# Scores of a gated recurrent layer: six levels of halving against three levels of quartering

## The chip, the cores and the metric

The kernel runs on one core of one Trainium2 chip. The metric is the device time of one execution in microseconds, lower is better; the median of three runs is 2374.85 us (2374.75 to 2374.86). Besides these runs there is one profiled execution, whose trace the profile and all rows below come from.

## The reference, cut to what matters

Two layers on 512 prompt frames and 32 sample frames of width 2048, 16 heads of 128. The first layer is an attention layer, the second a gated linear recurrence; the change lies in the second. Each layer has an input projection to four times the width and an output projection. In the recurrent layer a head's output is a sum over earlier frames, each weighted by a product of query and key and by the decay between the two frames:

```python
def hgrn2_chunk(S, inp):
    q, k, v, g = inp
    b = jnp.cumsum(g, axis=2)                                    # log decay, summed over the chunk
    o = jnp.einsum('bhtk,bhkv->bhtv', q * jnp.exp(b), S)         # what the state adds
    ...
    decay = jnp.exp(jnp.minimum(bs[:, :, :, :, None] - bs[:, :, :, None, :], 0.0))
    diag = jnp.einsum('bhaik,bhajk,bhaijk->bhaij', qs, ks, decay) * tri
    scores = off + jnp.einsum('bhaij,ac->bhaicj', diag, jnp.eye(n, dtype=diag.dtype))
    o = o + jnp.einsum('bhts,bhsv->bhtv', scores.reshape(bn, h, c, c), v)
    S_new = jnp.exp(b_last)[..., None] * S + jnp.einsum('bhsk,bhsv->bhkv', k * jnp.exp(jnp.minimum(b_last[:, :, None] - b, 0.0)), v)
    return S_new, o
```

The chunking is an identity of the mathematics; the kernel takes chunks of 128 frames. The exponent between a query and a key must never be positive, so a score can't be split into one factor of the query and one of the key over the whole chunk; it is split around a frame that lies between the two.

## The kernel before

**Projections.** Everything is kept transposed, 128 features on the partitions and 544 = 512 + 32 frames in the free dimension. A projection tile is 16 blocks of contraction; each is split in a rounded part and a remainder of weights and activations (`w_hi`, `w_lo`, `act_hi`, `act_lo`), and three products of 272 columns times two are summed (line 474). A tile is two halves of 8 blocks. One head needs four tiles, so eight halves, u = 0 to 7. Weights come in by SP's queue into a ring of four (`w_raw`); ACT rounds them (`hi`), DVE takes the difference (`lo`, line 1143), three halves ahead.

**The loop.** In the layer's loop over heads h = 0 to 14, PE computes half u of head h + 1 and after it the piece `rec_stage(h, u)` of head h. The last head, 15, has no half beside it; the first contraction blocks of the output projection, listed in `LAST_FILL`, are put between its pieces. DVE and ACT walk through the same u: first the weight split, then the evacuation of a projection tile (`evacuate`), then their part of head h (`rec_dve`, `rec_act`), then the start of head h + 1 (`rec_next`, and at u = 7 `rec_distances` and `rec_decays`). Each engine works in its written order; semaphores order the engines among each other.

**The levels.** The scores of a chunk are made by halving. At level m (64, 32, 16, 8, 4, 2) blocks of 2m frames are cut in two; the second half has the queries, the first the keys, and the decay is split at the first half's last frame. For a level DVE makes the differences of the summed log decays (`level(h, i, 0)`, lines 1265 and 1266, two instructions of 272 elements, 256 at the levels 64 and 32), ACT takes the exponential in place (`level_exp`, 544 or 512 elements), DVE multiplies with keys and queries (`level(h, i, 1)`, lines 1271 and 1272), and PE multiplies the two in full f32: one matmul of 64 columns for each of the four prompt chunks (line 595), and from m = 16 down one of 16 columns for the sample frames (line 599). A matmul in f32 stands as two records in the trace. `put` copies a level's scores under a mask into the score matrix `A`, with four or five COPY_PREDICATED (lines 1285 and 1292). The level m = 1 needs no matmul by chunk: products of neighbours, summed over the partitions by a matmul with ones (`pair`).

**What orders them.** Two buffers each for differences and products alternate (`dl`, `xl`), and two banks of PSUM, `M[1]` and `M[0]`, for the scores. PE's levels stand at u = 0 (m = 64), 1 (32), 2 (16), 3 (8 and 4) and 4 (2); at u = 5 PE multiplies `A` with the values. `r_x` tells PE that a level's products are there, `r_lev` tells DVE that its scores are, and `r_put` tells that they lie in `A`. The key and query products of the first two levels of a head are made at u = 7 of the head before, in `rec_distances`.

**Further names.** `own` is the diagonal score, with a remainder `own_lo` that PE waits for at u = 2; `kd` are the decayed keys for the state, turned by PE at u = 1; `S` is the state; `gate_r` the output gate. GpSimd (POOL) builds masks at the start, sums squares, and at the end of each layer takes the remainders `act_lo` of the first blocks of the output projection (line 450), while the last head is still in work.

Of the kernel before, what the change touches and what calls it, by code (L numbers as in the profile page):

```python
# [66 lines left out]
LEVELS = [64, 32, 16, 8, 4, 2, 1]  # L67
MASK_COL = {m: 64 * i for i, m in enumerate(LEVELS)}
# [37 lines left out]
def encoder_step(nc, x_prompt, x_sample, cache_k, cache_v, state_hgrn, norm_w, w_in, w_out, q_norm_w, k_norm_w,  # L106
# [4 lines left out]
    with ExitStack() as ctx:  # L111
# [26 lines left out]
        level_mask = sb("level_mask", [P, 64 * len(LEVELS)])  # L138
# [59 lines left out]
        qs, kk, qe, kd = c(T), c(T), c(T), c(T)  # L198
        eb = c(T)
        gate_r = g_tmp_r = c(T)  # L200
        dl = [c(T) for _ in range(2)]
        xl = [c(T) for _ in range(2)]
# [4 lines left out]
        o_cp, o_sq = xl  # L207
        o_hi, o_lo = [work_r(n, (4 * 2 + 2 + i) * T, T) for i, n in enumerate(("o_hi", "o_lo"))]
# [3 lines left out]
        pair = dl[0][:, 0:HT]  # L212
        pair_hi = work_r("pair_hi", (4 * 2 + 3) * T, HT)
        pair_lo = work_r("pair_lo", (4 * 2 + 3) * T + HT, HT)
# [74 lines left out]

        NL = len(LEVELS)  # L290

# [97 lines left out]
        def _(pool):  # L389
# [29 lines left out]
            for m in LEVELS:  # L419
                v = level_mask[:, MASK_COL[m]:MASK_COL[m] + 64].rearrange("p (b j) -> p b j", j=m)  # L420

                ch.done(pool.affine_select(out=v, in_=v, pattern=[[-2 * m, 64 // m], [0, m]], base=0,
                                           channel_multiplier=1, compare_op=ALU.is_ge, fill=0.0))
                ch.wait()
                ch.done(pool.affine_select(out=v, in_=v, pattern=[[2 * m, 64 // m], [0, m]], base=m - 1,
# [37 lines left out]
        def _(pe):  # L463
# [124 lines left out]
            def rec_level(h, i, bank):  # L588

                m = LEVELS[i]  # L590
                pe.wait_ge(r_x, h * NL + (i + 1))
                x = xl[i % 2]
                for b in range(NB):
                    rhs = x[:, b * P:(b + 1) * P].rearrange("p (b j) -> p b j", j=2 * m)[:, :, m:2 * m]
                    mm = pe.matmul(M[bank][:, b * 64:(b + 1) * 64], x[:, b * P:(b + 1) * P], rhs,  # L595
                                   start=True, stop=True)
                if m <= SAMPLE // 2:
                    rhs = x[:, SEQ:T].rearrange("p (b j) -> p b j", j=2 * m)[:, :, m:2 * m]
                    mm = pe.matmul(M[bank][:, 256:256 + SAMPLE // 2], x[:, LAST:T], rhs, start=True, stop=True)
                mm.then_inc(r_lev, 1)  # L600

            def rec_stage(h, u):
                if u == 2:
                    pe.wait_ge(kd_rows_cleared, 1)
                if u == 0:
                    if not (isinstance(h, int) and h == 0):
                        pe.wait_ge(r_orstd, h)
                    rec_level(h, 0, 1)
                elif u == 1:
# [6 lines left out]
                    rec_level(h, 1, 0)  # L616
# [520 lines left out]
        def _(dve):  # L1137
# [110 lines left out]
            def level(h, i, part):  # L1248
# [13 lines left out]
                if part == 0:  # L1262
                    if i >= 2:
                        dve.wait_ge(r_x, h * NL + (i - 1))
# [301 lines left out]
```

## Time and profile before

| | us |
|---|---|
| median of three runs | 2374.85 |
| the profiled execution's own time | 2374.45 |
| its span, first to last instruction | 2372.7 |
| PE busy in the span | 2333.4 (98%) |
| DVE busy | 1252.3 (53%) |
| ACT busy | 1021.1 (43%) |
| POOL busy | 96.2 (4%) |
| matmuls of the projections, line 474, three groups of 5120 | 1081.5 + 1063.1 + 1060.0 |
| matmuls of the levels, line 595, 768 records | 99.4 |
| the same for the sample frames, line 599, 128 records | 22.4 |

A record's duration reaches past the start of the next one, since matmuls are pipelined; so the sums of line 474 exceed the span, and what a matmul costs PE is read from one start to the next. DVE's and ACT's instructions overlap by about a tenth of a microsecond in the same way. Of the span, the part from 1237 to 2134 us is the loop of the recurrent layer, and 2134 to 2190 us its last head.

### The profile page before, as it was taken

To read this page: it belongs to the slowest core of one execution; us is meant where nothing else is said; L and a number is where in the kernel's file an instruction comes from. 1 tells how busy PE (TensorE), PEld (TensorE's weight loads), DVE (VectorE), ACT (ScalarE), POOL (GpSimd) and SP (SyncE) were. 2 spreads that over 40 slices of the span, in tenths; PEclk is the share of its full clock that TensorE was granted. 3 is DMA by queue.
4 is the path that set the end of the run, shared out by engine and by line. 5 is a ranking of instruction groups with operands and counts; after the bars stand their busy time and mean duration, and the time that the engine had idled before them with its cause. 6 is when DMAs were issued, how large, how long until landed. Compare 5 with 4: busy or idle time off the path is not lost. (4 is left out here: it accounts for less than half of the span.)

```text
span 2372.7 us, 46285 instructions
## 1 busy us (share of the span) xinstructions
PE 2333.4 (98%) x18457; PEld 2310.9 (97%) x18457; DVE 1252.3 (53%) x2278; ACT 1021.1 (43%) x1386; POOL 96.2 (4%) x95
## 2 busy tenths in 40 slices
PE   7999999999999999999999999999999999998999
PEld 6999999999999999899999999999999999997999
DVE  6444444444444444432357777777777777776221
ACT  5444444444444444532344444444444444444221
POOL 6000000000000000310100000000000000003000
PEclk9999999999999999999999999999999999998999
DMA  7333222222222222254532222222222222212542
GB/s 236 100 87 87 85 85 85 85 85 85 85 85 85 85 85 83 62 156 116 143 91 75 74 73 69 71 73 74 69 71 73 74 74 74 74 48 57 149 118 78
DMA packets 388088, 211.29 MB, mean 89 GB/s; under 512 B 9091, under 2 KB 378294, under 8 KB 388022
## 3 DMA queue, kind: packets, MB, share of 16 engines
q1 hardware_dynamic: 340182, 181.19, 26.8%
q10 hardware_dynamic: 47872, 29.64, 4.1%
q8 instruction: 22, 0.36, 0.1%
q14 instruction: 12, 0.10, 0.0%
HBM read 186.41 MB, written 24.38 MB: 89 GB/s over the span
## 5 line engine op out<-in xcount | busy, mean ns | idle before, releaser
L474 PE MATMUL psum<-act_hi,w_hi 128*128 128x272 f32 x5120 | 1081.5, 293 | 13.5 <-DVE act_lo L1152 5.3
L474 PE MATMUL psum<-act_hi,w_lo 128*128 128x272 f32 x5120 | 1063.1, 289 | 0.0
L474 PE MATMUL psum<-act_lo,w_hi 128*128 128x272 f32 x5120 | 1060.0, 289 | 0.0
L1143 DVE TENSOR_TENSOR w_lo<-w_raw,w_hi 128x1024 fp32r<-128x1024 f32 x320 | 400.5, 1252 | 859.3 <-ACT w_hi L785 859.2
L474 PEld LDWEIGHTS psum<-act_hi,w_hi 128*128 128x128 f32 x5120 | 805.7, 189 | 16.6 <-DVE act_lo L1152 4.4
L474 PEld LDWEIGHTS psum<-act_lo,w_hi 128*128 128x128 f32 x5120 | 807.9, 189 | 0.0
L474 PEld LDWEIGHTS psum<-act_hi,w_lo 128*128 128x128 f32 x5120 | 803.4, 190 | 0.0
L785 ACT ACTIVATE w_hi<-w_raw 128x1024 fp32r<-128x1024 f32 x320 | 338.0, 1057 | 680.8 <-PE psum L474 634.7
L785 ACT ACTIVATE work<-work 128x544 f32<-128x544 f32 (+2 forms) x368 | 261.4, 723 | 313.0 <-DVE work L1266 198.7
L785 ACT ACTIVATE work<-psum 128x512 f32<-128x512 f32 (+5 forms) x256 | 111.3, 483 | 148.8 <-PE psum L465 115.1
L450 POOL TENSOR_TENSOR act_lo<-full,act_hi 128x544 fp32r<-128x544 f32 x24 | 37.1, 1548 | 1905.5 <-DVE act_lo L1152 1876.5
L595 PE MATMUL psum<-work 128*128 128x64 f32 x768 | 99.4, 273 | 3.6 <-DVE work L1272 3.6
L595 PEld LDWEIGHTS psum<-work 128*128 128x128 f32 x768 | 95.6, 195 | 4.0 <-issue 2.3
L1160 DVE TENSOR_TENSOR Y<-psum,rstd_x 128x544 f32<-128x544 f32 x126 | 90.3, 717 | 8.7 <-ACT rstd_x L785 6.3
L785 ACT ACTIVATE work<-work,one_c 128x544 f32<-128x544 f32 (+1 forms) x80 | 78.2, 978 | 2.1
L1535 DVE TENSOR_TENSOR work<-psum,work 128x544 f32<-128x544 f32 x32 | 23.2, 724 | 92.6 <-PE psum L474 92.6
L785 ACT ACTIVATE work<-Y 128x1088 f32<-128x1088 f32 x64 | 56.3, 880 | 21.9 <-PE psum L577 21.9
L785 ACT ACTIVATE sp_hi<-work 128x1376 fp32r<-128x1376 f32 x32 | 43.4, 1355 | 48.1 <-DVE work L1196 46.6
L1285 DVE COPY_PREDICATED work<-level_mask,psum 128x64 f32<-128x64 int32 x384 | 60.9, 238 | 0.0
L465 PE MATMUL psum<-ident,work 128*128 128x128 f32 (+2 forms) x289 | 48.5, 277 | 6.6 <-DMA work<-in_hgrn_norm_w 3.8
L439 POOL TENSOR_TENSOR work<-work 128x544 f32<-128x544 f32 x32 | 47.1, 1472 | 169.0 <-ACT work L785 168.3
L1272 DVE TENSOR_TENSOR work<-work 128x272 f32<-128x272 f32 (+1 forms) x112 | 50.3, 449 | 0.0
(205 smaller groups left out, 1710.3 us busy)
## 6 DMA issues: line engine op xcount, KB each, us to landing
w_raw<-in_w_in SPq DMA_DIRECT2D x256, 512.0 KB, 4.0
w_raw<-in_w_out SPq DMA_DIRECT2D x64, 512.0 KB, 6.3
out<-work ACTq DMA_DIRECT2D x48, 256.0 KB, 2.4
x_residual<-work ACTq DMA_DIRECT2D x32, 272.0 KB, 3.8
work<-x_residual SPq DMA_DIRECT2D x32, 272.0 KB, 3.0
full<-in_x_prompt SPq DMA_DIRECT2D x3, 1024.0 KB, 11.5
work<-in_cache_k ACTq DMA_DIRECT2D x16, 128.0 KB, 2.3
work<-in_cache_v ACTq DMA_DIRECT2D x16, 128.0 KB, 4.1
```

The lines of the kernel that those rows point to most:

```text
L439: pool.tensor_tensor(sq_sum, sq_sum, squares, ALU.add).then_inc(x_summed, 1)
L450: pool.tensor_tensor(act_lo[:, k, :], full[:, k, :], act_hi[:, k, :].bitcast(F32), ALU.subtract).then_inc(act_lo_ready, 1)
L465: return pe.matmul(out, in_, ident[0:n, 0:n], is_transpose=True, start=True, stop=True, **kw)
L474: mm = pe.matmul(acc[par][:, j, :], w[:, slot, k % KH, :], a[:, k, j * HT:(j + 1) * HT], start=(k == 0 and n == 0), stop=(k == KT - 1 and ...
L595: mm = pe.matmul(M[bank][:, b * 64:(b + 1) * 64], x[:, b * P:(b + 1) * P], rhs, start=True, stop=True)
L785: return nc.scalar.activation(out, in_, f, **kw)
L1143: dve.tensor_tensor(w_lo[:, slot], w_raw[:, slot], w_hi[:, slot].bitcast(F32), ALU.subtract).then_inc(lo_ready, 1)
L1160: dve.tensor_tensor(Y[:, j, :].rearrange("p (a t) -> p a t", a=2), acc[j % 2], rstd_x[:].rearrange("p (a t) -> p a t", a=2), ALU.mult).the ...
L1272: dve.tensor_tensor(x2, cut(qs)[1], d2, ALU.mult).then_inc(r_x, 1)
L1285: ins = dve.copy_predicated(dst, msk, src)
L1535: dve.tensor_tensor(x_new[par].rearrange("p (a t) -> p a t", a=2), acc[par], x_old[par].rearrange("p (a t) -> p a t", a=2), ALU.add).then_ ...
```

## The change

The levels become groups of quartering: blocks of 4m frames with m = 32, 8, 2 are cut in four parts. The parts' keys are decayed to the end of their own part, once; the queries come in three sets, one for each of the three ends inside the block: 3m queries behind the first end, 2m behind the second, m behind the third, 6m columns for 4m frames. One matmul of 192 columns per chunk (48 for the sample frames) gives the scores of all three sets for a group; three groups with 24 + 4 records take the place of six levels with 48 + 8 records per head. The pairs of neighbours stay, made directly from `cum`, `qs` and `kk`.

```diff
-LEVELS = [64, 32, 16, 8, 4, 2, 1]
+GROUPS = [32, 8, 2]
+GROUP_COLS = 192
+BUF = T + 6 * T // 4
...
+            def rec_group(h, i):
+                n = in_group(i)[1]
+                pe.wait_ge(r_x, h * NL + (i + 1))
+                xk, xq = key_part(i), query_part(i)
                 for b in range(NB):
+                    at = (b % 2) * 256
+                    mm = pe.matmul(M[b // 2][:, at:at + GROUP_COLS], xk[:, b * P:(b + 1) * P],
+                                   xq[:, b * GROUP_COLS:(b + 1) * GROUP_COLS], start=True, stop=True)
...
+                ch.done(func(xk, xk, ACT.Exp))
+                func(xq, xq, ACT.Exp).then_inc(r_dexp, 1)
...
+            def group(h, i, part):
...
+                    ends = blocks(c)[:, :, m - 1:m].broadcast_to([P, 4 * segs, m])
+                    ch.done(dve.tensor_tensor(blocks(xk), ends, blocks(c), ALU.subtract))
+                    for b in range(3):
+                        end = c[:, :, (b + 1) * m - 1:(b + 1) * m].broadcast_to([P, segs, (3 - b) * m])
+                        ins = dve.tensor_tensor(xq[:, :, q_at[b]:q_at[b + 1]], c[:, :, (b + 1) * m:4 * m], end, ALU.subtract)
...
+                    ch.done(dve.tensor_tensor(xk[:, :, 0:3 * m], k[:, :, 0:3 * m], xk[:, :, 0:3 * m], ALU.mult))
+                    for b in range(3):
+                        v = xq[:, :, q_at[b]:q_at[b + 1]]
+                        ins = dve.tensor_tensor(v, q[:, :, (b + 1) * m:4 * m], v, ALU.mult)
...
+            def put(h, i, *between):
+                for b in range(3):
...
+                        dve.memset(tick, 0.0)
...
+                    on = msk[:, b, :].unsqueeze(1).unsqueeze(3).broadcast_to([P, NB, segs, w])
+                    ins = dve.copy_predicated(dst[:, :, :, (b + 1) * m:4 * m], on, scores[:, :, :, q_at[b]:q_at[b + 1]])
```

Each group's scores fill both `M[0]` and `M[1]`, so a group on PE waits until the one before lies in `A`. The three copies of `put` overlap in `A`, so each waits for the one before it, behind a MEMSET of one element that carries the wait or behind another instruction (the gate). The masks of POOL at the start become six short ones instead of fourteen, with 63 columns instead of 448. The buffers of the first group lie over `o_cp`, so `rec_distances` now waits for the head's output (`o_ready`) at its first instruction instead of ahead of its products. The order of the pieces on PE becomes: group 32 at u = 0, nothing at u = 1 and 2, group 8 at u = 3, group 2 at u = 4.

On PE, in the loop at u = 3, the levels m = 8 and m = 4 stood one behind the other, before:

```order
L591 REGISTER_ALU [waits r_own_scores_times_v]
L595 MATMUL psum<-work 128x64 [waits r_x]
L595 MATMUL psum<-work 128x64 x3
L599 MATMUL psum<-work 128x16
L591 REGISTER_ALU [waits r_scores_put]
L595 MATMUL psum<-work 128x64 [waits r_x]
L595 MATMUL psum<-work 128x64 x3
L599 MATMUL psum<-work 128x16
```

The same place now, up to the next half:

```order
L611 REGISTER_ALU [waits r_own_scores_times_v]
L615 MATMUL psum<-work 128x192 [waits r_x]
L615 MATMUL psum<-work 128x192 x3
L618 MATMUL psum<-work 128x48
L499 REGISTER_ALU
```

One group of wider matmuls stands where two levels stood, and the wait for `r_put` (named `r_scores_put`) between them is gone.

On DVE, in the loop at u = 4, behind the weight split (`w_lo`) and the evacuation (`Y`), before:

```order
L1160 TENSOR_TENSOR Y<-psum,rstd_x 128x544 [waits half_done]
L1285 COPY_PREDICATED work<-level_mask,psum 128x8x8 [waits r_level_scores,r_scores_put,consts_ready]
L1285 COPY_PREDICATED work<-level_mask,psum 128x8x8 x3
L1292 COPY_PREDICATED work<-level_mask,psum 128x2x8
L1268 REGISTER_ALU
L1271 TENSOR_TENSOR work<-work 128x136x2 [waits r_level_scores,r_dexp]
L1272 TENSOR_TENSOR work<-work 128x136x2
```

The same place now; line 1413 is the gate, line 1304 the differences of the pairs:

```order
L1177 TENSOR_TENSOR Y<-psum,rstd_x 128x544 [waits half_done]
L1304 TENSOR_TENSOR work<-work 128x272 [waits r_level_scores]
L1327 MEMSET small 128x1 [waits r_level_scores,r_scores_put,consts_ready]
L1334 COPY_PREDICATED work<-level_mask,psum 128x16x24
L1340 COPY_PREDICATED work<-level_mask,psum 128x24
L98 REGISTER_ALU
L1413 TENSOR_TENSOR work<-Y,work 128x544 [waits r_gate_sig,dve_chain]
L1334 COPY_PREDICATED work<-level_mask,psum 128x16x16
L1340 COPY_PREDICATED work<-level_mask,psum 128x16
L98 REGISTER_ALU
L1332 MEMSET small 128x1 [waits dve_chain]
L1334 COPY_PREDICATED work<-level_mask,psum 128x16x8
```

The products of level m = 2 stood behind the copies and PE waited for them; the products of group 2 now stand ahead, at the end of u = 3, and PE's group 2 waits for the last of these copies.

On DVE at u = 7, from the head's output (`full`) to the products of the next head's first level, before:

```order
L1398 TENSOR_TENSOR full<-work 128x544
L1265 TENSOR_TENSOR work<-work 128x4x64 [waits r_cum]
L1266 TENSOR_TENSOR work<-work 128x4x64
L1303 TENSOR_TENSOR work<-work 128x128 x4
L1303 TENSOR_TENSOR work<-work 128x32
L1265 TENSOR_TENSOR work<-work 128x8x32
L1266 TENSOR_TENSOR work<-work 128x8x32
L1268 ISA [waits o_ready,r_qk]
```

The same place now, with the products (line 1293 and below):

```order
L1445 TENSOR_TENSOR full<-work 128x544
L1286 TENSOR_TENSOR work<-work 128x512 [waits o_ready,r_cum]
L1289 TENSOR_TENSOR work<-work 128x4x96
L1289 TENSOR_TENSOR work<-work 128x4x64
L1289 TENSOR_TENSOR work<-work 128x4x32
L1356 TENSOR_TENSOR work<-work 128x128 x4
L1356 TENSOR_TENSOR work<-work 128x32
L1292 ISA [waits r_qk]
L1293 TENSOR_TENSOR work<-work 128x4x96 [waits r_dexp]
```

The differences of a second level, which stood between the first level's differences and its products, are gone; only the differences for `kd` are left between, and the wait for `o_ready` moved to the front.

## Rows read from the trace of the kernel before

**Rows 1.** Busy time by stretch, the loop: stretch and length, PE, PEld, DVE, ACT, POOL, clock.

```profile
1290.00:2140.00 850.00, 847.95 (x6862) 845.29 (x6861) 612.63 (x1461) 396.00 (x571) 0.00 (x0) 1.00 0.24 71
```

**Rows 2.** All waits of PE from 1225 to 2190 us: total, times, longest.

```profile
PE psum L628 <- DVE own_lo L1333: 5.2, 1, 5.2
PE psum L595 <- DVE work L1272: 3.6, 2, 2.1
PE psum L474 <- DVE act_lo L1152: 1.6, 1, 1.6
PE psum L660 <- DVE o_lo L1377: 1.4, 1, 1.4
```

**Rows 3.** Timeline of PE in the loop: start, us, line, operands, columns, records.

```profile
1613.56 0.39 PE L622 MATMUL psum<-work 128*128 128x128 f32 x2
1613.78 1.00 PE L595 MATMUL psum<-work 128*128 128x64 f32 x8
...
1621.61 1.00 PE L595 MATMUL psum<-work 128*128 128x64 f32 x8
1622.44 0.35 PE L599 MATMUL psum<-work 128*128 128x16 f32 x2
1622.64 1.08 PE L595 MATMUL psum<-work 128*128 128x64 f32 x8
...
1623.76 0.50 PE L474 MATMUL psum<-act_hi,w_hi 128*128 128x272 f32 x2
...
1629.86 1.00 PE L595 MATMUL psum<-work 128*128 128x64 f32 x8
...
1658.53 1.00 PE L595 MATMUL psum<-work 128*128 128x64 f32 x8
1659.34 0.50 PE L474 MATMUL psum<-act_hi,w_hi 128*128 128x272 f32 x2
```

**Rows 4.** Timeline of PE, a matmul of 512 columns in f32 between the layers.

```profile
1199.25 1.02 PE L719 MATMUL psum<-work,ones_r 128*128 128x512 f32 x2
1200.11 0.30 PE L720 MATMUL psum<-work,ones_r 128*128 128x32 f32 x2
```

**Rows 5.** Timeline of DVE in the loop, u = 4.

```profile
1622.90 1.22 DVE L1143 TENSOR_TENSOR w_lo<-w_raw,w_hi 128x1024 fp32r<-128x1024 f32 x1 [2.79 <-ACT w_hi L785]
...
1624.67 0.61 DVE L1285 COPY_PREDICATED work<-level_mask,psum 128x64 f32<-128x64 int32 x4
1625.19 0.17 DVE L1292 COPY_PREDICATED work<-level_mask,psum 128x16 f32<-128x16 int32 x1
1625.28 0.43 DVE L1271 TENSOR_TENSOR work<-work 128x272 f32<-128x272 f32 x1
1625.63 0.44 DVE L1272 TENSOR_TENSOR work<-work 128x272 f32<-128x272 f32 x1
```

**Rows 6.** Waits of DVE for itself in the layer: total, times, longest.

```profile
DVE work L1239 <- DVE work L1237: 2.3, 15, 0.2
```

**Rows 7.** Timeline of DVE and ACT at u = 7, around the first level.

```profile
1651.60 0.42 DVE L1265 TENSOR_TENSOR work<-work 128x256 f32<-128x256 f32 x1
...
1654.18 0.42 DVE L1272 TENSOR_TENSOR work<-work 128x256 f32<-128x256 f32 x1
...
1652.38 0.63 ACT L785 ACTIVATE work<-work 128x512 f32<-128x512 f32 x1 [4.20 <-DVE work L1266]
```

**Rows 8.** Costliest groups of the page, ACT's weight rounding: busy, mean ns, idle before.

```profile
L785 ACT ACTIVATE w_hi<-w_raw 128x1024 fp32r<-128x1024 f32 x320 | 338.0, 1057 | 680.8 <-PE psum L474 634.7
```

**Rows 9.** Timeline of the last head: POOL, DVE, PE.

```profile
2152.01 2.83 POOL L450 TENSOR_TENSOR act_lo<-full,act_hi 128x544 fp32r<-128x544 f32 x2 [2.16 <-ACT act_hi L785]
...
2153.57 1.85 DVE L1333 TENSOR_TENSOR own_lo<-work,own_hi 128x544 fp32r<-128x544 f32 x1
...
2169.99 1.27 PE L595 MATMUL psum<-work 128*128 128x64 f32 x8 [1.56 <-DVE work L1272]
```

**Rows 10.** Busy time in the last head behind the wait of 5.2 us, columns as rows 1.

```profile
2155.00:2162.00 7.00, 6.53 (x33) 6.33 (x34) 5.42 (x19) 2.41 (x4) 0.91 (x1) 0.61 0.52 151
```

More of the change, by code:

```diff
@@ L197, in encoder_step @@
         cum = c(T)
-        qs, kk, qe, kd = c(T), c(T), c(T), c(T)
+        qs, kk, qe = c(T), c(T), c(T)
         eb = c(T)
         gate_r = g_tmp_r = c(T)
-        dl = [c(T) for _ in range(2)]
-        xl = [c(T) for _ in range(2)]
+        at_bufs = c.at
+        assert 2 * BUF == 5 * T
+        bufs = [c(BUF) for _ in range(2)][::-1]
+        kd = bufs[1][:, 0:T]
+        tick = small[:, 7, 2:3]
         A = c(SEQ + SAMPLE)
@@ L206, in encoder_step @@
         S = c(6 * P).rearrange("p (b d) -> p b d", b=6)
-        o_cp, o_sq = xl
-        o_hi, o_lo = [work_r(n, (4 * 2 + 2 + i) * T, T) for i, n in enumerate(("o_hi", "o_lo"))]
+        o_cp, o_sq = [work[:, at_bufs + i * T:at_bufs + (i + 1) * T] for i in range(2)]
+        o_hi, o_lo = [work_r(n, at_bufs + (2 + i) * T, T) for i, n in enumerate(("o_hi", "o_lo"))]
         own = lse
@@ L1295, in rec_distances @@
             def rec_distances(h):
                 dve.wait_ge(r_cum, h + 1)
-                level(h, 0, 0)
+                if not (isinstance(h, int) and h == 0):
+                    dve.wait_ge(o_ready, h + H)
+                group(h, 0, 0)
                 for b in range(5):
@@ L1304, in rec_distances @@
                     ins.then_inc(r_kdx, 1) if b == NB else ch.done(ins)
-                level(h, 1, 0)
                 dve.wait_ge(r_qk, h + 1)
-                if not (isinstance(h, int) and h == 0):
-                    dve.wait_ge(o_ready, h + H)
-                level(h, 0, 1)
+                group(h, 0, 1)
                 dve.wait_ge(r_kde, h + 1)
                 dve.tensor_tensor(kd, kd, kk, ALU.mult).then_inc(r_kd, 1)
-                level(h, 1, 1)
             def rec_dve(h, u):
@@ L1333, in rec_dve @@
                     dve.tensor_tensor(own_lo, own, own_hi.bitcast(F32), ALU.subtract).then_inc(r_own_lo, 1)
-                    level(h, 4, 0)
+                    group(h, 1, 1)
                 elif u == 3:
@@ L1342, in rec_dve @@
                                       ).then_inc(r_own_v, 1)
-                    put(h, 2, 1)
-                    level(h, 4, 1)
-                    level(h, 5, 0)
+                    group(h, 2, 0)
                     dve.wait_ge(r_upd, h + 1)
```

207 lines of the change are left out of this document (111 added, 96 removed).

## The prediction

> **What bounds the kernel now.** I read the busy time by stretch first. In the loop of the recurrent layer PE is busy for 847.95 of 850 us at the full clock, DVE for 612.63, ACT for 396.00 [rows 1]. Then PE's waits: from the layer's first head to its end there are four entries, 11.8 us in all [rows 2], and all lie in the last head: of 1240 to 2134 us the same view is empty. So in the loop PE waits for nobody: a microsecond taken from PE in a head is a microsecond of the kernel as long as DVE and ACT keep ahead of it, and one added to DVE or ACT is free up to their lead. The last head is the opposite: there PE waits for DVE, and DVE's order counts. Hence three questions: what a head's scores cost PE, whether the lead holds in the loop, and what the last head does.
>
> **PE: the levels go.** A matmul in f32 is two records, so a level is 8 records of 64 columns, and from m = 16 down 2 more of 16. From start to start the first level takes 1659.34 - 1658.53 = 0.81 us [rows 3], the second repeats it. At u = 3 the first of the two takes 1622.64 - 1621.61 = 1.03 and the second 1623.76 - 1622.64 = 1.12; the levels at u = 2 and u = 4 repeat 1.03. A head: 2 x 0.81 + 3 x 1.03 + 1.12 = 5.83 us.
>
> **PE: the groups come.** A head now has 3 x 8 records of 192 columns and 2 x 2 of 48. No row has 192 columns in f32, so I price it between neighbours: 64 columns 0.10 each (0.81 / 8), 128 columns 0.11 ((1613.78 - 1613.56) / 2) [rows 3], 512 columns 0.43 ((1200.11 - 1199.25) / 2) [rows 4]. From 128 to 512 columns the slope is 0.32 / 384 = 0.83 ns per column; from 64 to 128 it is far flatter, so below 128 something other than the columns sets the pace, and at 128 the columns have caught up (128 x 0.83 = 0.107). For 192: 0.11 + 64 x 0.83 ns = 0.164. Bounds: 0.160 if only columns count; and, if what fills the 64-column record stays and columns are added to it, 0.104 + 128 x 0.83 ns = 0.211. I take 0.164, because 128 and 512 columns [rows 3, 4] lie on one line through almost zero, and the upper bound contradicts the row of 128 columns. The two records of 48 take the 0.20 of the two of 16 (1622.64 - 1622.44): 64 columns cost no more. A head: 24 x 0.164 + 2 x 0.20 = 4.34 us. The columns rise by half (1536 to 2304 prompt columns), the time falls, because half of the 64-column record was not columns.
>
> The saving is 5.83 - 4.34 = 1.49 us a head, in 15 heads of the loop 22.4 us. The changes between f32 and the other matmuls stay as many per head: each u keeps a piece in f32 except that u = 1 and u = 2 keep theirs without a level.
>
> **DVE and ACT: the work stays about equal.** DVE's price from start to start [rows 5]: 64 masked elements (0.52 / 4 = 0.13), 16 in 0.09, 272 in 0.35, on one line 0.065 + 1.05 ns per element. Before, a head has 28 + 1 instructions of 256 or 272 (29 x 0.35 = 10.1) and 28 copies (24 x 0.13 + 4 x 0.09 = 3.5), together 13.6 us. After: per group differences of 544, 408, 272 and 136 elements (0.64 + 0.49 + 0.35 + 0.21 = 1.69) and products of 408, 408, 272, 136 (1.54), three groups 9.7; pairs 3 x 0.35 = 1.05; copies per group of 384, 256 and 128 (0.47 + 0.33 + 0.20), for two groups 24, 16 and 8 besides (0.25): 3.5; MEMSETs and waits for its own copies (0.15 each, 2.3 / 15) [rows 6] about 1.5. Together 15.7, 2 us more on an engine that has (850 - 612.63) / 14, or 17 us a head, free. What counts is where. ACT: seven exponentials of some 540 elements become six of 408 and 816 and one of 272, elements 3744 to 3944: nothing.
>
> **Where the lead is thinnest.** First, u = 4. PE's group 2 overwrites both banks and so waits for the last copy of group 8. In times of the trace before: DVE starts the weight split at 1622.90 and its copies could start at 1624.67 [rows 5]. Now come the pairs' differences 0.35, a MEMSET 0.07, copies 0.47 + 0.09, a wait and the gate 0.15 + 0.64, copies 0.33 + 0.08, wait and MEMSET 0.22, copies 0.20 + 0.17: 2.8, done at 1627.4. PE ends the half of u = 3 at 1621.61, then group 8 (1.31 + 0.20), then the half of u = 4, 1629.86 - 1623.76 = 6.10: 1629.2. Lead 1.8 us, no wait.
>
> Second, the first group of the next head. The chain on DVE ran from 1651.60 to the last product's end at 1654.18 + 0.42 = 1654.60 [rows 7], PE came at 1658.53 [rows 3]: 3.9 us. Now: the wait for its own output 0.15, differences of 512, 384, 256, 128 (1.60), to 1653.4; then ACT: 512 elements last 0.63 [rows 7], 1024 last 1.06 [rows 8], 0.84 ns per element, so 384 and 768 are 0.52 + 0.85 with 0.1 overlapped, plus 0.1 to start: 1654.8. DVE fills only 0.9 of that with `kd`, waits 0.5, and multiplies for 1.47: 1656.3. Lead 2.2 us, no wait in the loop. The diagonal scores of u = 2 don't wait longer than before: `own_lo` now follows four differences (1.69) where a masked copy and two products stood (1.2).
>
> **The last head.** There nothing covers the second chain: PE waited 2.1 us for the first level [rows 2] and will wait 1.7 more. Then POOL is at work for `act_lo`, and DVE's instructions with two inputs slow down: `own_lo` took 1.85 us there [rows 9] against 0.64 by the line above. Before, four level instructions stood ahead of the weight split at u = 1 and two more before `own_lo`; now the gate and four differences stand there. Counting one and a half microseconds for each under POOL, `own_lo` comes about 2.5 us earlier, so the wait of 5.2 us shrinks to some 2.5. Later group 2 waits for copies that follow the weight split, where before the last products did, with a wait of 1.56 [rows 9]: PE comes there some 3 us earlier and waits about 2.5 us longer. Waits lower the clock: 0.61 of full speed behind the 5.2 us [rows 10]. I sum the last head to 0 with 4 us either way, its own 1.49 used up.
>
> **Sum.** Span 2372.7 - 22.4 = 2350.3; around it the profiled execution has 1.75 us (2374.45), and the median of the runs lies 0.4 above that: 2374.85 - 22.4 = **2352.5 us**. The shorter mask work of POOL at the start I cost at nothing, since PE and DVE wait there for the input frames.
>
> **The rivals.** *A record's fixed part stays under wide columns* (0.211): a head costs 24 x 0.211 + 0.40 = 5.46, saves 0.37, in 15 heads 5.5: 2369. Against it stands the row of 128 columns (0.11, not 0.157); 5%.
>
> The Trainium skill ("TensorE: Matmul & The Clock Gate", section "Part 3: Packing small matmuls — row/col tiling") says that a weight load overlaps running matmuls only where the row groups differ. All loads here use all rows, so by that rule each load would stand in front of its matmul, which is this rival and its 2369. The rows of 128 and 512 columns disagree with it; the same page's section "LDWEIGHTS (loading the stationary operand)" gives a load as columns / 1.2 ns, 107 ns for 128, which is close to the 0.10 of the narrow records, as a floor and not as an addend.
>
> *DVE is late at u = 4 in every head.* Masks broadcast along two axes and scores read in four-dimensional pieces have no row; if the copies cost 4 times my price per element, the 816 elements take 2.6 us longer, against a lead of 1.8: PE waits 0.8 a head. The clock then falls: at 0.61 over 7 us the loss is 0.39 x 7 = 2.7 us. 15 x (0.8 + 2.7) = 52 against 22.4: 2374.85 + 30 = 2405, slower. It decides from three times the price on. For it: no row has such a copy. Against: the masked copies of 64 and of 16 elements lie on the line of the plain ones. 7%, of it 2% with waits too short to turn the sign.
>
> *The last head eats part of it*: `own_lo` doesn't come earlier, the two later waits stay, and the clock is low longer: 2.5 + 1.7 + 2.7 = 7 us, 2359.5; 8%.
>
> **How the numbers follow.** Forecast 80%, with its own range 2348 to 2357 (price 0.160 gives 1.4 us less, last head 4 either way). With the last head's case, 88%: range 2347 to 2361; the two other cases lie outside. Two runs of this kernel differ by far less than 0.2% (4.7 us), which I take as what can be told from no change. Faster: 80 + 8 + 5 = 93%; slower 5%; between 2%.
>
> **What would show it.** Right: 384 records of 192 columns at 0.164 from start to start, 4.3 us of scores per head on PE, no wait of PE in the loop, 1.5 us less from head to head, PE's busy time lower by some 23 us, the last head's waits moved from `own_lo` to the first group and group 2. Wrong: records of 192 columns at 0.2 or more; PE waiting in the loop for line 1340 (copies) or 1296 (products); a granted clock below 1.00 in the loop; copies of 384 elements above 1 us.

## The result and the profile after

The changed kernel's median is 2343.26 us (2341.09 to 2343.76), beside 2374.8 us of the kernel before: a ratio of 0.9867, 95% interval 0.9855 to 0.9878. The direction was right; the time lies below the range's low end of 2347. The profiled execution, the fastest of its four, has a span of 2339.1 us, 33.6 less than before.

Where the 33.6 us lie is read from two rows of PE's timeline, the first and the last turn of `v` (transposing matmuls, line 465 before, 485 after): they stand ahead of head 0's pieces and ahead of the last head's, fifteen heads apart. Columns: start, us, engine, line, operands, columns, records. Before:

```profile
1230.40 0.71 PE L465 MATMUL psum<-ident,Y 128*128 128x128 f32 x5
...
2133.68 0.71 PE L465 MATMUL psum<-ident,Y 128*128 128x128 f32 x5
```

After, with the groups of one head between them:

```profile
1226.02 0.71 PE L485 MATMUL psum<-ident,Y 128*128 128x128 f32 x5
...
1582.55 1.46 PE L615 MATMUL psum<-work 128*128 128x192 f32 x8
1583.72 0.55 PE L494 MATMUL psum<-act_hi,w_hi 128*128 128x272 f32 x2
...
1590.34 0.50 PE L494 MATMUL psum<-act_hi,w_hi 128*128 128x272 f32 x2
...
1598.15 0.50 PE L494 MATMUL psum<-act_hi,w_hi 128*128 128x272 f32 x2
...
1604.25 1.46 PE L615 MATMUL psum<-work 128*128 128x192 f32 x8
1605.55 0.32 PE L618 MATMUL psum<-work 128*128 128x48 f32 x2
...
1611.79 1.46 PE L615 MATMUL psum<-work 128*128 128x192 f32 x8
...
2100.92 0.71 PE L485 MATMUL psum<-ident,Y 128*128 128x128 f32 x5
```

| us of the profiled execution | before | after | difference |
|---|---|---|---|
| up to the first turn | 1230.40 | 1226.02 | -4.4 |
| fifteen heads of the loop | 903.28 | 874.90 | -28.4 |
| behind the last turn, to the end | 239.02 | 238.18 | -0.8 |

A head takes 58.33 us instead of 60.22, 1.89 less; the prediction had 1.49. At u = 3 eight records of 192 columns take 1605.55 - 1604.25 = 1.30, so 0.1625 each. The loop, as rows 1 (stretch and length, PE, PEld, DVE, ACT, POOL, clock, and DMA share and GB/s, which aren't used):

```profile
1260.00:2080.00 820.00, 820.00 (x6467) 817.50 (x6467) 623.19 (x1333) 390.44 (x563) 0.00 (x0) 1.00 0.26 75
```

PE is still the bound, at the full clock; DVE's busy time is 44.3 us a head (623.19 / 820 x 58.33) instead of 43.4 ([rows 1], 612.63 / 850 x 60.22), 0.9 more where the prediction had 2. PE's waits from the layer's first head to the end of its last, as [rows 2]:

```profile
PE psum L644 <- DVE own_lo L1381: 4.1, 1, 4.1
PE psum L615 <- DVE work L1296: 3.8, 1, 3.8
PE psum L615 <- DVE work L1340: 3.0, 1, 3.0
PE psum L494 <- DVE act_lo L1169: 1.7, 1, 1.7
PE psum L674 <- DVE o_lo L1424: 0.9, 1, 0.9
```

All lie in the last head, none in the loop; together 13.5 us, where it was 11.8. The two thin leads, on DVE's timeline: the end of the first group's chain at u = 7 (as [rows 7]) and the copies of group 8 at u = 4 (as [rows 5]).

```profile
1579.29 1.09 DVE L1296 TENSOR_TENSOR work<-work 128x384 f32<-128x384 f32 x3
...
1607.67 0.59 DVE L1334 COPY_PREDICATED work<-level_mask,psum 128x384 f32<-128x384 int32 x1
...
1608.15 0.18 DVE L1340 COPY_PREDICATED work<-level_mask,psum 128x24 f32<-128x24 int32 x1
...
1609.75 0.16 DVE L1340 COPY_PREDICATED work<-level_mask,psum 128x8 f32<-128x8 int32 x1
```

The last copy ends at 1609.91 and PE comes to group 2 at 1611.79: a lead of 1.9 (predicted 1.8). The copy of 384 elements takes 0.48 from start to start (predicted 0.47). The first group's products end at 1580.38, PE comes at 1582.55: 2.2 (predicted 2.2).

So three differences ask for a cause: 0.40 us a head more than predicted, the start, and the last head, where little changed though its waits did.

### The profile page after: what moved, and what is told of

The parts are those of the page before. It is cut to its first block, busy times and chain, and to the rows that moved or that the text cites. A ratio compares the mean times of both kernels' runs of the same rounds, so it can differ in the third digit from the quotient of the medians.

```text
span 2339.1 us, 45080 instructions
## 1 busy us (share of the span) xinstructions
PE 2300.3 (98%) x18009; PEld 2277.7 (97%) x18009; DVE 1272.3 (54%) x2150; ACT 1018.9 (44%) x1386; POOL 91.8 (4%) x87
## 4 chain that ended last, share of the span: by engine, by line
PE 93%; DVE 2%; ACT 2%; issue 1%; ACTq 0%; DVEq 0%
PE psum L494 79%; PE psum L615 3%; PE psum L485 2%; PE psum L590 1%; PE psum L572 1%; PE psum L540 1%; PE psum L566 1%; ACT work L799 1%; PE psum L661 1%; ACT act_hi L799 1%; PE psum L640 1%; PE psum L663 0%; PE psum L522 0%; PE psum L521 0%; PE psum L546 0%
## 5 line engine op out<-in xcount | busy, mean ns | idle before, releaser
L799 ACT ACTIVATE work<-work 128x544 f32<-128x544 f32 (+6 forms) x368 | 256.5, 726 | 335.4 <-DVE work L1289 191.2
L615 PE MATMUL psum<-work 128*128 128x192 f32 x384 | 72.3, 332 | 6.8 <-DVE work L1296 3.8
L1334 DVE COPY_PREDICATED work<-level_mask,psum 128x384 f32<-128x384 int32 x144 | 68.2, 474 | 4.9 <-PE psum L618 2.2
L615 PEld LDWEIGHTS psum<-work 128*128 128x128 f32 x384 | 63.4, 193 | 7.3 <-issue 4.0
L799 ACT ACTIVATE sp_hi<-work 128x1376 fp32r<-128x1376 f32 x32 | 43.4, 1355 | 48.1 <-DVE work L1213 46.7
L1296 DVE TENSOR_TENSOR work<-work 128x408 f32<-128x408 f32 (+1 forms) x144 | 57.7, 457 | 0.0
L1289 DVE TENSOR_TENSOR work<-work 128x408 f32<-128x408 f32 (+1 forms) x144 | 56.4, 447 | 0.0
```

The source lines that it names most:

```text
L615: mm = pe.matmul(M[b // 2][:, at:at + GROUP_COLS], xk[:, b * P:(b + 1) * P], xq[:, b * GROUP_COLS:(b + 1) * GROUP_COLS], start=True, stop= ...
L799: return nc.scalar.activation(out, in_, f, **kw)
L1289: ins = dve.tensor_tensor(xq[:, :, q_at[b]:q_at[b + 1]], c[:, :, (b + 1) * m:4 * m], end, ALU.subtract)
L1296: ins = dve.tensor_tensor(v, q[:, :, (b + 1) * m:4 * m], v, ALU.mult)
L1334: ins = dve.copy_predicated(dst[:, :, :, (b + 1) * m:4 * m], on, scores[:, :, :, q_at[b]:q_at[b + 1]])
```

## Experiments

### Why a head saves 1.89 and not 1.49

Theory P is the prediction's own reading: a level costs what lies between its first record and the next matmul of a half. Theory H: that stretch leaves something out, since a half takes 6.10 us behind a piece in f32 and 6.02 behind the piece at u = 5, which ends in records of 272 columns like the half's own (means over the heads in both kernels). The data type alone doesn't make this difference: behind the pieces at u = 2 and u = 6, which end in records of the half's own kind (one record for a matmul) with 32 columns, a half takes 6.10 as well. To tell the theories apart, the piece at u = 0 was taken out of either kernel's loop (shown for the changed one; in the kernel before it is `rec_level(h, 0, 1)`). The last product but one of the half ahead gives `r_lev` (`early`), and the copies read other data, so the scores of the first group are left out. The kernels of this section and the next ran once each; their times from head to head are means over fifteen heads.

```diff
                 if u == 0:
                     if not (isinstance(h, int) and h == 0):
                         pe.wait_ge(r_orstd, h)
-                    rec_group(h, 0)
+                    if isinstance(h, int):
+                        rec_group(h, 0)
...
+                            if early is not None and (k, n, j) == (ks[-1], 2, 0):
+                                mm.then_inc(early, 1)
...
+                if i == 0 and not isinstance(h, int):
+                    scores = work[:, 4 * T:4 * T + NB * GROUP_COLS].rearrange("p (n x) -> p n x", n=NB)
```

> The kernel before without the matmuls of level m = 64 in the loop (the copies then put other data into A in their place); the half ahead of it gives the semaphore. So u = 0 has no piece in f32 between two halves. Read is the time from head to head (60.22 us in the kernel before). Theory P (the prediction's reading: a level costs what lies between its first record and the first matmul of the half behind it): 0.81 less, 59.41. Theory H (a piece in f32 costs more than that, because the half behind it takes 6.10 from its first to its last start and 6.02 where no piece in f32 stands ahead, as at u = 5): 0.89 less, 59.33, and the half behind the empty place takes 6.02.

> The changed kernel without the matmuls of group m = 32 in the loop (the copies take other data), the same edit on the other side. Read is the time from head to head (58.33 us in the changed kernel). The prediction's price, 8 x 0.164: 1.31 less, 57.02. Theory P read from the changed kernel's own trace (1.16 from the first record to the half behind it): 57.17. Theory H (1.16 and the longer half behind it, 6.16 against 6.02): 1.30 less, 57.03. If H holds on both sides, the prediction had the groups' price right and the levels' too low.

The timeline of PE in the kernel before: the half ahead of the level at u = 0 (line 474), the turn behind the next half (line 465), and the first matmuls of the halves at u = 2 and u = 3:

```profile
1592.23 0.50 PE L474 MATMUL psum<-act_hi,w_hi 128*128 128x272 f32 x2
...
1605.22 0.71 PE L465 MATMUL psum<-ident,work 128*128 128x128 f32 x5
...
1606.58 0.50 PE L474 MATMUL psum<-act_hi,w_hi 128*128 128x272 f32 x2
...
1615.51 0.50 PE L474 MATMUL psum<-act_hi,w_hi 128*128 128x272 f32 x2
```

The same without the level, with the first and the last turn:

```profile
1231.13 0.71 PE L465 MATMUL psum<-ident,Y 128*128 128x128 f32 x5
...
1587.71 0.50 PE L474 MATMUL psum<-act_hi,w_hi 128*128 128x272 f32 x2
...
1599.82 0.71 PE L465 MATMUL psum<-ident,work 128*128 128x128 f32 x5
...
2121.41 0.71 PE L465 MATMUL psum<-ident,Y 128*128 128x128 f32 x5
```

The two halves with the level take 1605.22 - 1592.23 = 12.99, without it 1599.82 - 1587.71 = 12.11: 0.88, though only 0.81 lie between first record and next half [rows 3]. From head to head it is (2121.41 - 1231.13) / 15 = 59.35, 0.87 less than 60.22: nearer to H's 0.89 than to P's 0.81. The changed kernel without its first group:

```profile
1227.36 0.71 PE L485 MATMUL psum<-ident,Y 128*128 128x128 f32 x5
...
2082.66 0.71 PE L485 MATMUL psum<-ident,Y 128*128 128x128 f32 x5
```

855.30 / 15 = 57.02, 1.31 less than 58.33: the prediction's 8 x 0.164 to the hundredth, where P from this kernel's rows (1583.72 - 1582.55 = 1.17) is 0.14 short. So the groups were priced right and the levels too low.

How much too low, records of 96 and of 64 columns tell (each matmul of 192 cut in two, in three):

```diff
-                    mm = pe.matmul(M[b // 2][:, at:at + GROUP_COLS], xk[:, b * P:(b + 1) * P],
-                                   xq[:, b * GROUP_COLS:(b + 1) * GROUP_COLS], start=True, stop=True)
+                    for n0 in range(0, GROUP_COLS, 64):
+                        mm = pe.matmul(M[b // 2][:, at + n0:at + n0 + 64], xk[:, b * P:(b + 1) * P],
+                                       xq[:, b * GROUP_COLS + n0:b * GROUP_COLS + n0 + 64], start=True, stop=True)
```

> The changed kernel with each score matmul of 192 columns cut into two of 96 with the same keys. Columns stay, records double (from 24 to 48 per head besides the sample frames'). Theory floor (a record of up to some 128 columns costs 0.104 whatever it holds, the reason for the change's gain): 48 x 0.104 = 5.0 in place of 24 x 0.1625 = 3.9, 1.1 us more per head, 16 us in the loop, about 2358 to 2361. Theory columns (only columns cost): no change, within 2 us of the changed kernel.

> The changed kernel with each score matmul of 192 columns cut into three of 64, columns next to each other. Theory floor: 72 x 0.104 = 7.5 in place of 3.9, 3.6 us more per head, 54 us in the loop, about 2396 to 2400, slower than the kernel before, so that quartering with narrow matmuls would lose. Theory columns: no change. It also tells whether the 0.115 from record to record of the levels m = 4 and below came from their strided columns: then 0.104 here.

PE's timeline with 96 columns, the turns and u = 0:

```profile
1227.80 0.71 PE L485 MATMUL psum<-ident,Y 128*128 128x128 f32 x5
...
1593.08 1.92 PE L616 MATMUL psum<-work 128*128 128x96 f32 x16
1594.78 0.50 PE L494 MATMUL psum<-act_hi,w_hi 128*128 128x272 f32 x2
...
2124.58 0.71 PE L485 MATMUL psum<-ident,Y 128*128 128x128 f32 x5
```

And with 64:

```profile
1228.75 0.71 PE L485 MATMUL psum<-ident,Y 128*128 128x128 f32 x5
...
1610.12 2.79 PE L616 MATMUL psum<-work 128*128 128x64 f32 x24
1612.72 0.50 PE L494 MATMUL psum<-act_hi,w_hi 128*128 128x272 f32 x2
...
2165.75 0.71 PE L485 MATMUL psum<-ident,Y 128*128 128x128 f32 x5
```

The heads take 59.79 and 62.47 us, 1.46 and 4.14 more than 58.33, and the kernels 2366.1 and 2409.86 us, the second slower than before. With 24 x 0.1625 = 3.90 taken away and 48 or 72 records put in, a record of 96 costs (3.90 + 1.46) / 48 = 0.112 and one of 64 costs (3.90 + 4.14) / 72 = 0.112. "Only columns cost" is out, and so is my floor of 0.104, by which 2358 to 2361 and 2396 to 2400 were expected. The pieces at u = 0 show why I read too little: 8, 16 and 24 narrow records take 0.81 [rows 3], 1.70 and 2.60 up to the next half, 0.112 for each further record and a fixed 0.09 less; the half behind gives that back. The single records of the trace show where. At u = 0 of the kernel before, the level's records start 0.110 to 0.112 apart, but the second only 0.056 behind the first, and the half 0.084 behind the last; within the half the second record then starts 0.211 behind the first, where 0.125 is its step. So 0.08 or 0.09 of the level's time stand within the half.

The levels that no experiment took out cost the same. From the first matmul of the half at u = 2 to that of the half at u = 3 there were 1615.51 - 1606.58 = 8.93, and now, with ten narrow records gone and nothing in their place, 1598.15 - 1590.34 = 7.81. Over all heads (means of fifteen, from half to half):

| us | u = 0 | u = 1 | u = 2 | u = 3 | u = 4 | u = 5 to 7 |
|---|---|---|---|---|---|---|
| before | 6.90 | 7.46 | 8.93 | 8.25 | 7.14 | 21.08 |
| after | 7.27 | 6.62 | 7.81 | 7.54 | 7.54 | 21.08 |
| narrow records out | 8 | 8 | 10 | 20 | 10 | 0 |
| records of 192 and of 48 columns in | 8 + 0 | 0 | 0 | 8 + 2 | 8 + 2 | 0 |

At u = 2 that is 1.11 for ten records, 0.111 each, where the prediction read 1.03 for the same level. At u = 1 it is 0.84 for eight, and 0.89 with the 0.05 or 0.06 that the half there has become longer behind the records of 192 columns (6.16 instead of 6.10). Inside both levels of u = 3 the records start 0.112 apart; the 0.115 read there holds a first step of 0.139, behind a record of 16 columns. In the cut groups the columns lay next to each other, so 0.112 needs no stride to explain it.

### The lead at u = 4

```diff
                     pairs(h, 0)
+                    if not isinstance(h, int):
+                        for n in range(6):
+                            ch.done(dve.tensor_tensor(spare[:], cum[:, 0:384], cum[:, 0:384], ALU.subtract))
+                            ch.wait()
                     put(h, 1, gate_out)
```

> The changed kernel with two more instructions on DVE at u = 4 of every head in the loop, ahead of the copies of group 8, each 384 elements and a wait for itself, together about 1.2 us. Theory lead (the last copy is done 1.9 us before PE comes to group 2): no wait of PE in the loop, head to head 58.33, time within the changed kernel's runs. Rival: the lead is smaller than it looks, because DVE's later work of the head comes later too and another place waits: more than 58.4 from head to head.

> The same with six such instructions, about 3.7 us. Theory lead: DVE is 1.8 us late at group 2 in every head and PE waits for the copies. The prediction's rival of that kind priced a wait with a low clock behind it, 0.39 of 7 us or 2.7 us: 1.8 + 2.7 = 4.5 us a head, 67 us in all, about 2411. Without a fall of the clock: 1.8 a head, 27 us, about 2370. Rival: the wait shifts DVE and PE against each other and other waits follow: more than 70 us.

With two, a head takes 58.33 as without (2344.25 us in all) and PE has no wait in the loop: the lead is more than those 1.2 us. With six, 2372.81 us. PE's waits in the loop:

```profile
PE psum L616 <- DVE work L1341: 24.5, 15, 1.6
```

Busy time by stretch there, columns as above:

```profile
1300.00:2100.00 800.00, 778.75 (x6117) 773.61 (x6116) 633.69 (x1340) 367.77 (x530) 0.00 (x0) 1.00 0.25 73
```

And the turns on PE's timeline:

```profile
1227.72 0.71 PE L486 MATMUL psum<-ident,Y 128*128 128x128 f32 x5
...
2131.01 0.71 PE L486 MATMUL psum<-ident,Y 128*128 128x128 f32 x5
```

A head takes 60.22: 1.89 more, against 1.8 of a late DVE. PE waits for the copies once in each of 15 heads, 1.6 us each (24.5 of the 15 x 1.89 = 28.4 us show as waits), and the granted clock stays at 1.00. So the rival of a late DVE was priced wrongly: its 2.7 us of low clock per head did not come with a wait of this length, twice its 0.8. Being 1.8 us late in every head would have eaten just the whole gain of the loop, not turned it into 30 us of loss.

### The start

The masks of POOL had been costed at nothing, and the profiled execution begins the layer 4.4 us earlier. Two kernels move that load: the kernel before with its fourteen selects behind the sums of squares, and the changed kernel with eight more selects ahead of them.

```diff
-            for m in LEVELS:
-                v = level_mask[:, MASK_COL[m]:MASK_COL[m] + 64].rearrange("p (b j) -> p b j", j=m)
...
             for n in range(KT):
                 add_squares(n, (x_sq, x_sq_b)[n % 2])
+            for m in LEVELS:
+                v = level_mask[:, MASK_COL[m]:MASK_COL[m] + 64].rearrange("p (b j) -> p b j", j=m)
...
+            pool.memset(one_late[:], 1.0).then_inc(masks_ready, 1)
```

```diff
+            for m in (64, 32, 16, 8):
+                v = spare[:].rearrange("p (b j) -> p b j", j=m)
...
             pool.wait_ge(ident_ready, 1)
             ch.done(pool.tensor_copy(neg_tri[:], tri_f))
```

> The kernel before, with POOL's fourteen mask selects (and they alone) moved behind its sixteen sums of squares; the mask copies wait for a semaphore of their own. Theory A (the changed kernel's shorter masks are what gained time at the start: POOL comes to the sums earlier, they no longer bunch beside DVE's first differences of the weights, and PE's wait of 3.8 us for the weight remainder at 19 us shrinks to about 0.7): 2 to 4.4 us less than before, so 2370.5 to 2373, and the first level of the recurrent layer 2 to 4.4 us earlier than at 1236.98. Theory B (the start differs by when the input frames land, and the masks have no part in it, as the prediction costed them): 2374.8 within 0.5, the wait for the weight remainder stays at 3 to 4 us.

> The changed kernel with the old load on POOL at the start: eight more selects, of 64 columns on a tile that nobody reads, so fourteen selects ahead of the sums of squares as in the kernel before. Theory A (masks at the start cost time): 2 to 4 us more than the changed kernel beside it, so about 2345 to 2347, and PE's wait for the weight remainder near 19 us is back at some 3 us. Theory B (masks have no part): the changed kernel's time within 0.7 us, wait 0.7 us as in the changed kernel.

> The changed kernel unaltered, so that the three kernels beside it have its times on the same chip. Both theories: a median between 2341 and 2344 us, as its runs so far. If the kernel's own runs differ by the start alone (between 1.5 and 4.4 us gained there), the span of its profiled execution follows the time of PE's first group of the recurrent layer one for one.

The unaltered kernel, run beside them, has 2344.02 us (2343.08 to 2344.57), its first turn at 1229.96, and 874.91 and 237.93 us in the other two stretches: nearly all of the difference between two executions of one kernel lies ahead of the layer. In a third one the first turn was at 1228.84. So of the 4.4 us a good part is scatter. The masks moved away gave 2373.11 beside 2374.35 (ratio 0.9994, interval 0.9985 to 1.0003), the masks put back 2343.18 beside the unaltered 2344.02, with the wrong sign: neither can be told from nothing. PE's wait for the weight remainder went as theory A says, from 3.8 to 0.5 us with the masks moved away and to 2.5 with them put back, but the unaltered changed kernel has 0.7, 2.3 and 1.0 in its three traces.

What differs between two executions can be seen, and it is two things. The first: POOL and DVE around the second weight remainder (line 1160), first in the profiled execution, whose remainder began first:

```profile
15.44 3.52 POOL L459 TENSOR_TENSOR work<-work 128x544 f32<-128x544 f32 x2 [1.25 <-ACT work L799]
...
15.05 1.21 DVE L1160 TENSOR_TENSOR w_lo<-w_raw,w_hi 128x1024 fp32r<-128x1024 f32 x1
```

then in the second one, where the sum of squares began first:

```profile
15.94 1.37 POOL L459 TENSOR_TENSOR work<-work 128x544 f32<-128x544 f32 x1 [0.76 <-ACT work L799]
...
16.04 2.35 DVE L1160 TENSOR_TENSOR w_lo<-w_raw,w_hi 128x1024 fp32r<-128x1024 f32 x1
```

Whichever begins first runs at its own pace and the other waits for it; PE waited 0.7 us for the remainder in the one and 2.3 in the other. A wait on POOL that lets the remainder go first was tried:

```diff
             for n in range(KT):
+                if n == 2:
+                    pool.wait_ge(lo_ready, 2)
                 add_squares(n, (x_sq, x_sq_b)[n % 2])
```

> The changed kernel with one more wait on POOL at the start: the third sum of squares waits until DVE has the second half's weight remainder. In the profiles so far that remainder took 2.35 us where POOL's third sum had begun just before it, and 1.21 where it had not. Theory collision (this is what the start's scatter of some 4 us comes from): the remainder takes 1.21 in every run, PE's wait for it is 0.5 to 1.1 us, and the median falls from some 2344 to 2341 or 2342. Rival (the scatter comes from when the input frames and weights land, and the collision only moves to the next remainder of the activations): the same median as the unaltered kernel beside it within 0.7 us, with the same scatter.

> The changed kernel unaltered, for comparison with the kernel beside it on the same chip: 2343 to 2344.5 as before, from head to head 58.33, and the scatter of its runs, 1.5 to 3 us, all of it ahead of the recurrent layer.

The remainder took 1.21 and PE waited 0.6, but the first turn came at 1228.80, and the medians are 2342.71 (2341.76 to 2343.71) against 2344.34 (2342.46 to 2345.2): 1.6 lower, between the two forecasts, and the runs overlap. The collision is real but isn't all of the scatter.

The second thing is the granted clock. Near 50 us PE waits for the remainder `act_lo` (line 1473). The first matmuls behind that wait and the busy time around it, columns as above, in the profiled execution:

```profile
51.76 0.52 PE L494 MATMUL psum<-act_hi,w_hi 128*128 128x272 f32 x2 [2.36 <-DVE act_lo L1473]
...
46.00:61.00 15.00, 12.64 (x95) 11.90 (x95) 12.30 (x20) 8.21 (x14) 3.79 (x3) 1.00 0.48 149
```

and in the second one:

```profile
54.29 0.82 PE L494 MATMUL psum<-act_hi,w_hi 128*128 128x272 f32 x2 [2.37 <-DVE act_lo L1473]
...
46.00:61.00 15.00, 12.63 (x82) 11.52 (x80) 12.12 (x17) 7.54 (x11) 4.81 (x3) 0.89 0.39 126
```

The wait is the same, 2.4 us; in the one the granted clock stays at 1.00, in the other it is at its lower level, 1.2 GHz, for a part of the stretch and 0.89 in the mean. From the 145th to the 193rd record of the projections it is 9.73 us in the one and 11.14 in the other. All fourteen traces have this wait, 2.3 to 2.5 us. In four the clock stayed up and those 48 records took 9.73 to 9.76; in ten, the kernel before among them, it fell and they took 11.1 to 11.4. From there to the first turn every trace has 1169.4 to 1170.2 us, so the scatter arises in the first 61 us.

The 4.4 us between the profile before and the one after are with this: 3.1 for the weight remainder (PE waits 3.8 before, 0.7 after), 1.5 for the clock that fell in one and not in the other, less 0.3 for the first projection matmul, which came earlier before, and 0.1 elsewhere. Both of the larger parts also come and go between executions of the one changed kernel.

### The last head

```diff
-                    group(h, 1, 0)
                     dve.wait_ge(r_own_hi, h + 1)
                     dve.wait_ge(r_own_prod, h + 1)
                     dve.tensor_tensor(own_lo, own, own_hi.bitcast(F32), ALU.subtract).then_inc(r_own_lo, 1)
+                    group(h, 1, 0)
...
-                    if u == 4 - l:
+                    if u == 4:
                         lo(g0 + 4, 0)
```

> The changed kernel with two moves on DVE: own_lo stands ahead of the four differences of group 8 (in every head), and in the last head the weight difference for a half of the output projection that is needed only 20 us later stands behind the copies of group 8 instead of ahead of them. Theory A (the last head is bound by DVE from the diagonal on: it idles for less than 3 us between 2104 and 2137 us): PE's wait of 4.05 us for own_lo goes, but what follows waits as much longer for group 8's products, and only the moved weight difference counts: its 1.2 us off the wait of 3.01 for the copies; last head 1 to 2 us shorter. Theory B (PE's waits there are what costs, and the low clock behind them): the 4.05 us go and the clock stays up, last head 3 to 5 us shorter. In the loop neither expects a change, since own_lo has a lead there. Rival C: the group's products come 0.7 us later and this is late in every head: some 10 us slower.

PE's waits with both moves:

```profile
PE psum L615 <- DVE work L1389: 4.9, 1, 4.9
...
PE psum L615 <- DVE work L1340: 2.2, 1, 2.2
...
PE psum L644 <- DVE own_lo L1380: 0.2, 1, 0.2
```

The 4.0 to 4.2 us for `own_lo` in the three traces of the unaltered kernel shrink to 0.2, and u = 3 waits 4.9 us instead, for the diagonal's product with the values (line 1389), which stands behind group 8's products on DVE. The 3.0 to 3.4 us for the copies shrink to 2.2. Behind the last turn remain 237.70 us against 237.93 to 238.18 of the unaltered kernel: 0.2 to 0.5 us, theory A, with less than its 1 to 2. A head of the loop takes 58.33 as without, so rival C is out. The medians, 2342.25 and 2344.02, differ by no more than the starts do. DVE is the bound there. The timeline of DVE and POOL in the changed kernel's last head:

```profile
2114.52 1.87 DVE L1286 TENSOR_TENSOR work<-work 128x544 f32<-128x544 f32 x1
2116.31 3.40 DVE L1289 TENSOR_TENSOR work<-work 128x408 f32<-128x408 f32 x3
...
2109.91 9.30 POOL L470 TENSOR_TENSOR act_lo<-full,act_hi 128x544 fp32r<-128x544 f32 x5 [932.32 <-DVE act_lo L1169]
```

And its busy time by stretch:

```profile
2116.00:2126.00 10.00, 5.95 (x27) 5.56 (x26) 9.25 (x13) 2.96 (x5) 5.89 (x4) 0.67 0.28 86
```

Three differences of 408 elements and less take 3.40 us beside POOL's remainders, where three products of 384 and less take 1.09 in the loop; DVE is busy 9.25 of 10 us while PE is for 5.95, at a mean clock of 0.67.

## Why the prediction was right or wrong

- **The bound in the loop**: right. PE has no wait there before or after, and what was taken from PE is the kernel's gain.
- **The groups' price**: right. 0.1625 for a record instead of 0.164; a first group taken out is worth 1.31, as summed. 24 x 0.1625 and 4 x 0.112 make 4.35, against 4.34.
- **The levels' price**: the step that failed, a term of the sum that was mis-sized. "From start to start the first level takes 0.81 us" took the start of the half behind it for the end of the level. Taking the first level out is worth 0.87 to 0.88, ten records at u = 2 are worth 1.11 instead of 1.03, and a narrow record costs 0.112. 56 of them make 6.25 (56 x 8.04 / 72) where the sum had 5.83: five of the six levels were read 0.08 or 0.09 too short. 6.25 - 4.35 = 1.90 against a measured 1.89, and 15 x 0.40 = 6.0 us is the loop's whole miss. A row was there: the second level of u = 3 took 1.12 [rows 3], ten records at their full price; I kept it as a peculiarity of that level. And the two prices were got in unlike ways: the groups by a slope, which is free of what happens at the ends, the levels by one stretch, which is not. The group's price was held open (0.160 in the range, 0.211 as a rival), the level's was not.
- **The rival of the fixed part** (0.211, 2369): refuted by the records. A floor it is, not an addend: 0.112 at 64 and 96 columns, 0.11 at 128, 0.1625 at 192. The Trainium skill's rule that weight loads overlap running matmuls only where row groups differ ("TensorE: Matmul & The Clock Gate", "Part 3: Packing small matmuls — row/col tiling", which also names a background weight buffer as a second way) doesn't describe these records. The prediction set this rule equal to the rival of 0.211, which it is not. The Trainium skill's 107 ns for a load of 128 columns (same page, "LDWEIGHTS (loading the stationary operand)") would make a record of 192 columns 0.107 + 192 x 0.83 ns = 0.27 by that rule (an estimate); as a floor it is near the measured 112 ns of a narrow record; that the load is what sets the floor was not shown.
- **DVE's leads**: right, 1.9 and 2.2 us; the copies' price line held for pieces with more dimensions. The rival that lived from them didn't occur, since a copy of 384 takes 0.48; a late DVE makes PE wait as it said, but its clock term was wrong (1.00 behind waits of 1.6 us).
- **The last head**: right in size (0 with 4 either way, measured -0.8 with what follows it) and half right in kind. The first group's wait grew to 3.8 as summed (2.1 + 1.7). PE still waits 4.1 for `own_lo` where 2.5 was expected. `own_lo` itself came as summed: counted from the last turn, PE goes on behind it at 2120.40 - 2100.92 = 19.5 us instead of 2155.47 - 2133.68 = 21.8, 2.3 earlier (summed about 2.5). But PE, with one group where three levels stood and a longer first wait, also comes to that place 1.2 us earlier, and the sum took the whole 2.5 off the wait. The rival that the last head eats part of the gain didn't come: the waits took 1.7 us more (13.5 instead of 11.8), and the stretch behind the last turn is still 0.8 shorter.
- **The start at nothing**: open for 1 to 2 us. The 4.4 us of the profiles are the wait for the weight remainder and the clock, which differ between executions of one kernel too. Behind the first turn 29.2 us are gained in the profiled executions; the medians differ by 30.3 to 31.5 in three comparisons, so 1 to 2 us more lie ahead of it. The nine traces with the changed kernel's start have their first turn at 1226.0 to 1230.0, 1228.4 in the mean, the two with the start of the kernel before at 1230.4 and 1231.1, which agrees. The masks could be the cause, but the two kernels that moved them didn't show it.

2374.85 less the forecast's 22.4, the levels' 6.0 and the 0.8 behind the loop is 2345.6, already below the range's end of 2347; the 1 to 2 us ahead of the layer make most of the rest.

## What to carry to other kernels

Price what is removed in the same way as what is added: by the step per record between pieces of different length, not by the stretch from a piece's start to its neighbour's, since the neighbour behind can pay part of it. A record in f32 has a floor of 0.112 us here up to some 128 columns, so few wide matmuls beat many narrow ones even with half as many columns again; cut to 64 columns the same algorithm loses. And before an improvement is read off one profile, look at how far two executions of the same kernel differ in the stage in which it lies, and what clock was granted there in each.

## What the runs showed of the hardware

- A narrow piece in f32 takes 0.112 us for each record less 0.09 up to the next matmul of the projections, and the half of 48 records behind it takes 6.10, against 6.02 behind records of 272 columns; the difference lies in the half's first step (0.211 instead of 0.125).
- POOL and DVE, both with two inputs from SBUF: the one that begins first runs unhindered (the weight remainder 1.21), the other is held for the whole of it (2.35). The Trainium skill says the same ("SBUF — State Buffer", "SBUF: two separate sides": the shared ports are locked for a whole instruction and not divided), and these rows agree; which came first was chance here, and 0.1 us of order decided over 1.1.
- A wait of 1.6 us in every head left the granted clock at 1.00. Behind one of 2.4 us at the start it stayed at 1.00 in four traces and fell in ten (0.89 from 46 to 61 us in all of these), which cost 1.4 to 1.6 us. In the last head, with waits of 3 to 4 us close together, it was 0.67 on average over ten microseconds.
